# The way into the seven products: S blocks rounded ahead of the silu, rests in the order of use, one output half moved up

## The chip, the cores and the metric

The kernel runs on one core of one Trainium2 chip. The metric is the device time of the whole program in microseconds (us). Before the change three runs gave 2737.22, 2741.45 and 2741.87 us, median 2741.45 us.

## What is computed

Two blocks in sequence over 512 tokens of width 1024: a block with an HGRN/pool mixer and a forgetting-attention mixer, and a block with gated linear attention, retention and four SwiGLU feed-forward stages. The change lies in the feed-forward stages alone:

```
D_FF = 2816
def swiglu(x, w_in, w_out):
    gate, up = jnp.split(x @ w_in, 2, axis=-1)
    return (jax.nn.silu(gate) * up) @ w_out
# in second_block, twice for each of two layers:
h = layer_norm(DN_ALPHA * h + 0.5 * swiglu(h, ffn_w_in[i, j], ffn_w_out[i, j]), ...)
```

Everything is float32. The kernel makes a float32 product of three fast ones: each operand is rounded (its "hi"), the rest is the difference ("lo"), and hi\*hi + lo\*hi + hi\*lo are summed in PSUM.

## The kernel before

**Stages and rounds.** The four feed-forward stages are called ffn00, ffn01, ffn10 and ffn11. Each has ROUNDS = 11 rounds r; a round covers 256 hidden columns in two halves, s = 0 and 1, whose weights are the pieces a (s = 0) and b (s = 1). I write a2 for the piece a of round 2. The output weights of a round are its piece o; the products with them are issued one round later, so o1 is multiplied behind a2 and b2. Pieces are loaded by SyncE into a ring of SLOTS = 3 buffers (`sync_piece`, L300), a load waiting until the piece three places before has given its rests (`w_lo`).

**Two ways to multiply.** Rounds 0 and 1 are plain. From round SEVEN = 2 on, a half is seven block products after Strassen and Winograd (`tensor_seven`, L876) instead of eight: in the order of PRODUCTS (L835) A11, S2, S1, S3, A12, S4, A22, numbered x = 0 to 6. Each is 12 matmuls of 128 x 256. S1 to S4 are sums of weight blocks, made by GpSimd in `gpsimd_sums` (L985), four TENSOR_TENSORs at L991 to L996 that read and write SBUF. ScalarE rounds all four in one instruction (`scalar_unit_s`, L1021), VectorE makes the rests in two instructions of two blocks each (`vector_unit_s`, L1045) and then raises `w_s`. The sums of the next half may overwrite the one buffer `sums` only after that.

**Behind the products.** VectorE combines the products from PSUM: `vector_mid` step 0 gives f_u (L1065), step 1 gives f_e (L1068), step 2 gives f_g (L1071, L1072); product x = 4 waits for f_u, x = 5 for f_e, x = 6 for f_g. `vector_c11` (L1078) and `vector_c12` (L1084) finish two blocks, ScalarE takes their silu (`scalar_products`, L1115), and VectorE multiplies (`vector_products`, L1092 and twice L1097) and raises f_h. Then ScalarE rounds the hidden values (L542) and VectorE makes their rest (`vector_hidden_split`, L548), which sets oh_lo.

**Output products.** `tensor_out` (L436 to L438) makes eight tiles j of 6 matmuls of 128 x 512 in four PSUM banks. The first half of tiles 0 to 3 comes first, then their second half; tile 4 waits until VectorE has added tile 0 to the accumulator (`vector_outs_ffn`, L530 in round 1, L532 later, event acc), tile 5 waits for tile 1, and so on.

**What sets the order.** Every engine executes its instructions in the order written out by hand. For VectorE in the first seven-product round that is `vector_seventh` (L1216), for ScalarE the branch `r == SEVEN` in `scalar_ffn` (L1164). In this round (r = 2) the S blocks of a3 are rounded behind the silu of b2, and their rests are made behind the multiplications of b2; for b2 itself `tensor_seven` waits at x = 1 for `w_s`, that is for all four rests (L886). From round 3 on another loop takes over, which the change does not touch.

Of the kernel before, what the change touches and what calls it, by code (L numbers as in the profile page):

```python
# [7 lines left out]
F32 = mybir.dt.float32  # L8
# [6 lines left out]
MULT, ADD, SUB, MAX, MIN = ALU.mult, ALU.add, ALU.subtract, ALU.max, ALU.min  # L15

P = 128
T = 512
# [105 lines left out]
SEVEN = 2  # L124
# [113 lines left out]
def buffer(n):  # L238

    return n % SLOTS  # L240
# [103 lines left out]
def vector_piece_half(k, n, c):  # L344
    k.nc.vector.wait_ge(*k.at("w_hi", n))
    x = slice(c * D, (c + 1) * D)
    ins = k.nc.vector.tensor_tensor(k.lo(n)[:, x], k.w_raw[:, buffer(n), x], k.hi(n)[:, x].bitcast(F32), SUB)
    if c == 1:
        ins.then_inc(*k.up("w_lo", n))
# [479 lines left out]

H_BLOCK = {"B11": (0, 0), "B12": (0, 1), "B21": (1, 0), "B22": (1, 1)}  # L830
T_BLOCK = {"T2": 0, "T4": 1, "T3": 2}
S_BLOCK = {"S3": 0, "S1": 1, "S4": 2, "S2": 3}


PRODUCTS = (("A11", "B11", 0), ("S2", "T2", 1), ("S1", "T1", 2), ("S3", "T3", 3),  # L835
# [40 lines left out]
def tensor_seven(k, stage, r, s):  # L876

    pe, n, prior = k.nc.tensor, AT[stage, "ab"[s], r], before_seven(stage, r, s)
    pe.wait_ge(*k.at("w_lo", n))
    for x, (a, b, bank) in enumerate(PRODUCTS):  # L880
        if x < 4:
            event = ("f_p1", "f_c11", "f_c12", "f_c21")[x]
            pe.wait_ge(*(k.at(event, prior) if prior else k.at("f_h", (stage, r - 1, 1))))
        else:
            pe.wait_ge(*k.at(("f_u", "f_e", "f_g")[x - 4], (stage, r, s)))
        if x == 1 and r == SEVEN:  # L886
            pe.wait_ge(*k.at("w_s", n))
        if x == 1 and not prior:
            pe.wait_ge(*k.at("t_lo", (stage, "T3")))
        if x == 2 and not prior:  # L890
            pe.wait_ge(*k.at("t_lo", (stage, "T1")))
        (wh, wl), (xh, xl) = w_block(k, n, a), h_block(k, stage, b)
        for kk in range(4):
            w = slice(kk * P, (kk + 1) * P)
            ins = three(k, k.bank[bank][:, 0:256], wh[:, w], wl[:, w], xh[:, kk, :], xl[:, kk, :],
                        kk == 0, kk == 3)
        if x < 6:
            ins.then_inc(*k.up("f_p", (stage, r, s, x)))
    ins.then_inc(*k.up("used", n))
# [107 lines left out]
def scalar_unit_a22(k, n):  # L1007
    sc = k.nc.scalar
    sc.wait_ge(*k.at(f"loaded{buffer(n)}", n))
    sc.wait_ge(*k.at("used", BEFORE[n]))  # L1010
    sc.activation(wide_view(w_blocks(k, n, "A22", 1)[0]), raw_block(k, n, 1, 1), ACT.Copy
                  ).then_inc(*k.up("u_hi", (n, "A22")))


def scalar_unit_s(k, n):

    sc, (stage, what, r) = k.nc.scalar, PIECES[n]
    sc.wait_ge(*k.at("sums", n))
    if what == "a" and r > SEVEN:
        sc.wait_ge(*k.at("f_p", (stage, r - 1, 1, 1)))  # L1020
    sc.activation(w_blocks(k, n, "S", 4)[0], k.sums, ACT.Copy).then_inc(*k.up("u_hi", (n, "S")))  # L1021
# [12 lines left out]
def vector_unit_a22(k, n):  # L1034
    ve = k.nc.vector
    ve.wait_ge(*k.at("u_hi", (n, "A22")))
    hi, lo = (wide_view(x) for x in w_blocks(k, n, "A22", 1))
    ve.tensor_tensor(lo, raw_block(k, n, 1, 1), hi.bitcast(F32), SUB)


def vector_unit_s(k, n, half):
    ve, x = k.nc.vector, slice(half * 2 * T, (half + 1) * 2 * T)
    ve.wait_ge(*k.at("u_hi", (n, "S")))
    hi, lo = (w[:, x] for w in w_blocks(k, n, "S", 4))
    ins = ve.tensor_tensor(lo, k.sums[:, x], hi.bitcast(F32), SUB)  # L1045
    if half:
        ins.then_inc(*k.up("w_s", n))


def vector_unit_a1(k, n):  # L1050
# [24 lines left out]
def vector_c11(k, stage, r, s):  # L1075
    ve, key, p1 = k.nc.vector, (stage, r, s), k.f_h[:, s, HALF[0]]
    ve.wait_ge(*k.at("f_p", key + (4,)))
    ve.tensor_tensor(p1, p1, k.bank[1][:, 0:256], ADD).then_inc(*k.up("f_c11", key))  # L1078
# [30 lines left out]
def scalar_products(k, stage, r, s):  # L1109

    sc, key = k.nc.scalar, (stage, r, s)
    for t in range(2):
        sc.wait_ge(*k.at(("f_c11", "f_c12")[t], key))
        x = k.f_h[:, s, HALF[t]]
        sc.activation(x, x, ACT.Silu).then_inc(*k.up(("f_x1", "f_x2")[t], key))  # L1115
# [18 lines left out]
def scalar_ffn(k, stage):  # L1134
    sc, B = k.nc.scalar, FFN_NEXT[stage]
    sc.preload_act_table(ACT.Silu)
    scalar_piece(k, AT[stage, "a", 1])
    scalar_t(k, stage, "T2")
    scalar_hidden(k, stage, 0, 0)
    scalar_piece(k, AT[stage, "b", 1])  # L1140
    scalar_hidden_split(k, stage, 0, 0)
    scalar_t(k, stage, "T4")
    scalar_hidden(k, stage, 0, 1)
    scalar_hidden_split(k, stage, 0, 1)
    scalar_piece(k, AT[stage, "o", 0])
    scalar_t(k, stage, "T3")
    scalar_hidden(k, stage, 1, 0)
    n = AT[stage, "a", SEVEN]
    scalar_unit_a22(k, n)
    scalar_hidden_split(k, stage, 1, 0)  # L1150
    scalar_hidden(k, stage, 1, 1)
    scalar_unit_s(k, n)
    scalar_hidden_split(k, stage, 1, 1)
    scalar_unit_a1(k, n)
    scalar_t(k, stage, "T1")
    n = AT[stage, "b", SEVEN]
    scalar_unit_a22(k, n)
    for r in range(SEVEN, ROUNDS):
        last = r == ROUNDS - 1
        if r > SEVEN:  # L1160
            scalar_piece(k, AT[stage, "o", r - 1])
        scalar_first(k, stage, r, 0)
        scalar_unit_a1(k, AT[stage, "b", r])
        if r == SEVEN:  # L1164
            scalar_piece(k, AT[stage, "o", r - 1])
            scalar_unit_s(k, n)
            scalar_products(k, stage, r, 0)
            scalar_first(k, stage, r, 1)
            scalar_hidden_split(k, stage, r, 0)
            n = AT[stage, "a", r + 1]  # L1170
            scalar_unit_a22(k, n)
            scalar_products(k, stage, r, 1)
            scalar_unit_s(k, n)
            scalar_hidden_split(k, stage, r, 1)
            scalar_unit_a1(k, n)
            n = AT[stage, "b", r + 1]
            scalar_unit_a22(k, n)
            scalar_unit_s(k, n)
            continue
        scalar_products(k, stage, r, 0)  # L1180
        scalar_hidden_split(k, stage, r, 0)
        if not last:
            n = AT[stage, "a", r + 1]
            scalar_unit_a22(k, n)
            scalar_first(k, stage, r, 1)
            scalar_unit_s(k, n)
        else:
            scalar_first(k, stage, r, 1)
            scalar_piece(k, AT[stage, "o", r])
        scalar_products(k, stage, r, 1)  # L1190
        if last:
            sc.preload_act_table_set(EXP_LN)
        scalar_hidden_split(k, stage, r, 1)
        if not last:
            scalar_unit_a1(k, n)
            n = AT[stage, "b", r + 1]
            scalar_unit_a22(k, n)
            scalar_unit_s(k, n)
        elif B != "end":
            scalar_piece(k, HEAD[B][0])  # L1200
            scalar_piece(k, HEAD[B][1])
    scalar_exit(k, B)
# [9 lines left out]
def vector_hidden_split(k, stage, r, s):  # L1212
    vector_split(k, s, k.f_h[:, s, :], (stage, r, s), *ffn_oh(k, stage, r))


def vector_seventh(k, stage):  # L1216


    r = SEVEN
    n, n_o = AT[stage, "b", r], AT[stage, "o", r - 1]  # L1220
    vector_unit_a22(k, n)
    vector_mid(k, stage, r, 0, 0)
    vector_mid(k, stage, r, 0, 1)
    vector_unit_a1(k, n)
    vector_mid(k, stage, r, 0, 2)
    vector_piece_half(k, n_o, 0)
    vector_c11(k, stage, r, 0)
    vector_unit_s(k, n, 0)
    vector_c12(k, stage, r, 0)
    vector_unit_s(k, n, 1)  # L1230
    vector_products(k, stage, r, 0)
    k.nc.vector.wait_ge(*k.at("f_h", (stage, r, 0)))
    vector_mid(k, stage, r, 1, 0)
    vector_hidden_split(k, stage, r, 0)
    vector_mid(k, stage, r, 1, 1)
    vector_piece_half(k, n_o, 1)
    vector_mid(k, stage, r, 1, 2)
    n = AT[stage, "a", r + 1]
    vector_unit_a22(k, n)
    vector_c11(k, stage, r, 1)  # L1240
    vector_c12(k, stage, r, 1)
    vector_products(k, stage, r, 1)
    vector_unit_s(k, n, 0)
    vector_unit_s(k, n, 1)
    vector_hidden_split(k, stage, r, 1)
    vector_outs_ffn(k, stage, r - 1, range(2))
    vector_unit_a1(k, n)
    vector_outs_ffn(k, stage, r - 1, range(2, 4))
    n = AT[stage, "b", r + 1]
    vector_unit_a22(k, n)  # L1250
    vector_unit_s(k, n, 0)
    vector_outs_ffn(k, stage, r - 1, range(4, 6))
    vector_unit_s(k, n, 1)
    vector_outs_ffn(k, stage, r - 1, range(6, 8))
# [2315 lines left out]
```

## Time and profile before

| | us |
|---|---|
| median of three runs | 2741.45 |
| lowest, highest run | 2737.22, 2741.87 |
| span of the profiled execution | 2737.2 |
| TensorE matmul busy | 2660.2 (97%) |
| VectorE busy | 1940.6 (71%) |
| ScalarE busy | 1067.6 (39%) |
| GpSimd busy | 579.8 (21%) |
| mean granted TensorE clock | 0.994 |

The profiled execution is as long as the lowest of the three runs; nothing measurable lies around its span. Busy time of TensorE is the union of its matmuls, which overlap, so a pause shows best as the distance between the starts of two neighbours. In a timeline row the first number is the start in us from the start of the span, the second the duration, and a bracket at the end names idle time in front and what ended it. The engines are PE (TensorE), DVE (VectorE), ACT (ScalarE), POOL (GpSimd).

### The profile page before, as it was taken

The numbers are of one execution on the slowest core, as the hardware profiler recorded it, in microseconds if no ns is written. First come the engines' busy times: TensorE is split into PE (matmuls) and PEld (weight loads), VectorE is DVE, ScalarE is ACT, GpSimd is POOL, SyncE is SP. The second block draws the span as 40 slices with busy tenths as digits, with TensorE's granted clock in tenths as the row PEclk, the third lists the DMA queues.
The fourth block names the chain that finished last, engine by engine and source line by source line (L and its number), as shares of the span: only waits on it lengthen the run. The fifth ranks groups of instructions, "written<-read, shape, count | busy, mean of one in ns | idle before, by whom it ended". The sixth has DMA issues, their size and how long they took to land.

```text
span 2737.2 us, 38521 instructions
## 1 busy us (share of the span) xinstructions
PE 2660.2 (97%) x15927; PEld 2302.7 (84%) x15927; DVE 1940.6 (71%) x2634; ACT 1067.6 (39%) x1518; POOL 579.8 (21%) x370
## 2 busy tenths in 40 slices
PE   7999999999999999999999999999999999999998
PEld 5778877678899998888899988999978778788997
DVE  6888744556887875448888788888744644888887
ACT  4444455553443335343333334433322222344342
POOL 2111000011434300001444214433000000044430
PEclk9999999999999999999999999999999999999999
DMA  8444221212333332221433323332423213233331
GB/s 278 141 145 125 78 62 62 63 61 78 95 122 93 107 94 78 93 62 62 124 93 111 113 71 123 93 108 93 135 77 108 76 65 106 62 108 93 97 119 47
DMA packets 289856, 268.32 MB, mean 98 GB/s; under 512 B 10566, under 2 KB 256592, under 8 KB 288400
## 3 DMA queue, kind: packets, MB, share of 16 engines
q1 hardware_dynamic: 286448, 256.98, 30.1%
q0 software_dynamic: 2368, 6.64, 0.7%
q8 instruction: 126, 2.06, 0.3%
q10 hardware_dynamic: 864, 2.23, 0.3%
q14 instruction: 50, 0.41, 0.0%
HBM read 263.72 MB, written 2.10 MB: 97 GB/s over the span
## 4 chain that ended last, share of the span: by engine, by line
PE 74%; DVE 16%; ACT 4%; issue 3%; POOL 1%; DMA 0%; SPq 0%; DVEq 0%; ACTq 0%; POOLq 0%
PE psum L355 13%; PE psum L357 12%; PE psum L356 12%; PE psum L436 6%; PE psum L437 6%; PE psum L438 6%; PE psum L413 2%; PE psum L415 2%; PE psum L414 2%; DVE w_lo L340 2%; DVE acc L532 2%; DVE w_lo L1045 1%; PE psum L3266 1%; DVE stat L681 1%; PE psum L2810 1%
## 5 line engine op out<-in xcount | busy, mean ns | idle before, releaser
L355 PE MATMUL psum<-h_hi,w_hi 128*128 128x256 f32 (+1 forms) x2288 | 739.0, 323 | 19.2 <-DVE f_cffn L1065 6.5
L357 PE MATMUL psum<-h_hi,w_lo 128*128 128x256 f32 (+1 forms) x2288 | 720.6, 315 | 0.0
L356 PE MATMUL psum<-h_lo,w_hi 128*128 128x256 f32 (+1 forms) x2288 | 720.3, 315 | 0.0
L355 PEld LDWEIGHTS psum<-h_hi,w_hi 128*128 128x128 f32 x2288 | 438.5, 192 | 54.8 <-issue 13.8
L356 PEld LDWEIGHTS psum<-h_lo,w_hi 128*128 128x128 f32 x2288 | 438.7, 192 | 28.7 <-issue 5.1
L357 PEld LDWEIGHTS psum<-h_hi,w_lo 128*128 128x128 f32 x2288 | 438.3, 192 | 27.1
L991 POOL TENSOR_TENSOR val<-w_raw 128x512 f32<-128x512 f32 x72 | 100.6, 1398 | 1353.6 <-DMA w_raw<-in_ffn_w_in 948.5
L340 DVE TENSOR_TENSOR w_lo<-w_raw,w_hi 128x2048 fp32r<-128x2048 f32 x101 | 229.6, 2286 | 150.7 <-ACT w_hi L335 141.2
L532 DVE SCALAR_TENSOR_TENSOR acc<-psum,acc 128x512 f32<-128x512 f32 x416 | 270.0, 679 | 43.4 <-PE psum L438 43.4
L335 ACT ACTIVATE w_hi<-w_raw 128x2048 fp32r<-128x2048 f32 x104 | 197.1, 1910 | 140.1 <-PE psum L438 69.0
L355 PE MATMUL psum<-t_hiffn,w_hi 128*128 128x256 f32 x864 | 245.2, 284 | 3.4 <-DVE w_lo L1045 2.2
L356 PE MATMUL psum<-t_loffn,w_hi 128*128 128x256 f32 x864 | 244.5, 283 | 0.0
L357 PE MATMUL psum<-t_hiffn,w_lo 128*128 128x256 f32 x864 | 244.5, 283 | 0.0
L1045 DVE TENSOR_TENSOR w_lo<-val,w_hi 128x1024 fp32r<-128x1024 f32 x144 | 174.6, 1215 | 24.9 <-ACT w_hi L1021 24.1
L1115 ACT ACTIVATE consts<-consts 128x256 f32<-128x256 f32 x144 | 58.3, 418 | 318.6 <-DVE consts L1078 298.7
L355 PEld LDWEIGHTS psum<-t_hiffn,w_hi 128*128 128x128 f32 x864 | 165.8, 192 | 4.9 <-issue 2.9
L356 PEld LDWEIGHTS psum<-t_loffn,w_hi 128*128 128x128 f32 x864 | 165.8, 192 | 0.0
L357 PEld LDWEIGHTS psum<-t_hiffn,w_lo 128*128 128x128 f32 x864 | 165.8, 192 | 0.0
L994 POOL TENSOR_TENSOR val<-w_raw 128x512 f32<-128x512 f32 x72 | 161.4, 2242 | 0.0
L1021 ACT ACTIVATE w_hi<-val 128x2048 fp32r<-128x2048 f32 x72 | 137.9, 1915 | 38.8 <-POOL val L996 32.3
L335 ACT ACTIVATE w_hiffn<-w_raw 128x2048 fp32r<-128x2048 f32 x40 | 76.5, 1912 | 128.6 <-PE psum L438 128.6
L436 PE MATMUL psum<-w_hiffn,f_oh_hiffn 128*128 128x512 f32 x320 | 125.8, 393 | 0.0
(433 smaller groups left out, 5431.9 us busy)
## 6 DMA issues: line engine op xcount, KB each, us to landing
w_raw<-in_ffn_w_in SPq DMA_DIRECT2D x176, 512.0 KB, 5.0
w_raw<-in_ffn_w_out SPq DMA_DIRECT2D x88, 512.0 KB, 6.2
w_raw<-in_ret_w_in SPq DMA_DIRECT2D x48, 512.0 KB, 4.6
ada_raw<-in_ada_w SPq DMA_DIRECT2D x32, 512.0 KB, 4.5
w_raw<-in_odd_w_in SPq DMA_DIRECT2D x32, 512.0 KB, 5.0
w_raw<-in_even_w_in SPq DMA_DIRECT2D x24, 512.0 KB, 7.1
w_raw<-in_gla_w_in SPq DMA_DIRECT2D x24, 512.0 KB, 4.7
ada_first<-in_ada_w SPq DMA_DIRECT2D x8, 1024.0 KB, 9.6
```

Source lines behind the costliest of these rows:

```text
L335: k.nc.scalar.activation(k.hi(n), k.w_raw[:, buffer(n), :], ACT.Copy).then_inc(*k.up("w_hi", n))
L340: k.nc.vector.tensor_tensor(k.lo(n), k.w_raw[:, buffer(n), :], k.hi(n).bitcast(F32), SUB).then_inc(*k.up("w_lo", n))
L355: k.nc.tensor.matmul(out, ws, xs, start=first, stop=False)
L356: k.nc.tensor.matmul(out, ws, xl, start=False, stop=False)
L357: return k.nc.tensor.matmul(out, wl, xs, start=False, stop=last)
L436: k.nc.tensor.matmul(o, hi[:, c, x], k.hi(n)[:, w], start=first, stop=False)
L437: k.nc.tensor.matmul(o, lo[:, c, x], k.hi(n)[:, w], start=False, stop=False)
L438: return k.nc.tensor.matmul(o, hi[:, c, x], k.lo(n)[:, w], start=False, stop=last)
L532: ins = k.nc.vector.scalar_tensor_tensor(dst, b, 1.0, dst, MULT, ADD)
L994: po.tensor_tensor(sum_block(k, "S3"), a11, a21, ADD).then_inc(*k.pool.up())
L1021: sc.activation(w_blocks(k, n, "S", 4)[0], k.sums, ACT.Copy).then_inc(*k.up("u_hi", (n, "S")))
L1045: ins = ve.tensor_tensor(lo, k.sums[:, x], hi.bitcast(F32), SUB)
```

## The change

Four things, all of them in or in front of round 2 or 3 of each feed-forward stage.

1. The blocks S1 to S4 lie in the order S3, S4, S1, S2, and `vector_unit_s` makes the rests of S1 and S2 first (step 0), then those of S3 and S4 (step 1). Each step raises `w_s`. In round 2 TensorE waits at x = 1 for step 0 and at x = 3 for step 1.
2. ScalarE rounds the S blocks of a3 ahead of the silu of b2.
3. VectorE makes the rests of a3's S blocks ahead of c11 and c12 of b2, and no longer behind the multiplications.
4. The second half of o1's rests (`vector_piece_half`) comes ahead of step 1 of `vector_mid` for b2, in the place of the rest of the first hidden half, which moves behind c12.

```
-S_BLOCK = {"S3": 0, "S1": 1, "S4": 2, "S2": 3}
+S_BLOCK = {"S3": 0, "S4": 1, "S1": 2, "S2": 3}
...
-        if x == 1 and r == SEVEN:
-            pe.wait_ge(*k.at("w_s", n))
+        if r == SEVEN and x in (1, 3):
+            pe.wait_ge(*k.at("w_s", (n, "S1 S2") if x == 1 else n))
...
-def vector_unit_s(k, n, half):
-    ve, x = k.nc.vector, slice(half * 2 * T, (half + 1) * 2 * T)
+def vector_unit_s(k, n, step):
+
+    ve, x = k.nc.vector, slice((1 - step) * 2 * T, (2 - step) * 2 * T)
     ve.wait_ge(*k.at("u_hi", (n, "S")))
     hi, lo = (w[:, x] for w in w_blocks(k, n, "S", 4))
-    ins = ve.tensor_tensor(lo, k.sums[:, x], hi.bitcast(F32), SUB)
-    if half:
-        ins.then_inc(*k.up("w_s", n))
+    ve.tensor_tensor(lo, k.sums[:, x], hi.bitcast(F32), SUB).then_inc(*k.up("w_s", n if step else (n, "S1 S2")))
...
             n = AT[stage, "a", r + 1]
             scalar_unit_a22(k, n)
+            scalar_unit_s(k, n)
             scalar_products(k, stage, r, 1)
-            scalar_unit_s(k, n)
             scalar_hidden_split(k, stage, r, 1)
...
     vector_mid(k, stage, r, 1, 0)
-    vector_hidden_split(k, stage, r, 0)
+    vector_piece_half(k, n_o, 1)
     vector_mid(k, stage, r, 1, 1)
-    vector_piece_half(k, n_o, 1)
     vector_mid(k, stage, r, 1, 2)
     n = AT[stage, "a", r + 1]
     vector_unit_a22(k, n)
+    vector_unit_s(k, n, 0)
+    vector_unit_s(k, n, 1)
     vector_c11(k, stage, r, 1)
     vector_c12(k, stage, r, 1)
+    vector_hidden_split(k, stage, r, 0)
     vector_products(k, stage, r, 1)
-    vector_unit_s(k, n, 0)
-    vector_unit_s(k, n, 1)
     vector_hidden_split(k, stage, r, 1)
     vector_outs_ffn(k, stage, r - 1, range(2))
     vector_unit_a1(k, n)
```

## Rows read from the trace of the kernel before

**Rows 1.** The page's busy times: engine, us, share of the span, instructions.
```profile
PE 2660.2 (97%) x15927; PEld 2302.7 (84%) x15927; DVE 1940.6 (71%) x2634; ACT 1067.6 (39%) x1518; POOL 579.8 (21%) x370
```

**Rows 2.** Waits of PE: waiting line, releaser, us in total, times, longest.
```profile
PE psum L355 <- DVE f_cffn L1065: 6.5, 4, 1.6
```

**Rows 3.** Timeline of PE, stage ffn00, rounds 2 and 3.
```profile
715.20 0.28 PE L355 MATMUL psum<-h_hi,w_hi 128*128 128x256 f32 x1
...
717.34 0.35 PE L355 MATMUL psum<-t_hiffn,w_hi 128*128 128x256 f32 x1 [0.55 <-DVE w_lo L1045]
...
718.85 0.28 PE L355 MATMUL psum<-h_hi,w_hi 128*128 128x256 f32 x1
...
720.29 0.28 PE L355 MATMUL psum<-t_hiffn,w_hi 128*128 128x256 f32 x1
...
725.07 0.39 PE L355 MATMUL psum<-t_hiffn,w_hi 128*128 128x256 f32 x1 [0.30 <-DVE f_cffn L1072]
...
732.19 0.50 PE L436 MATMUL psum<-w_hiffn,f_oh_hiffn 128*128 128x512 f32 x1
...
737.77 0.28 PE L355 MATMUL psum<-h_hi,w_hi 128*128 128x256 f32 x1
...
745.32 0.38 PE L355 MATMUL psum<-h_hi,w_hi 128*128 128x256 f32 x1 [1.64 <-DVE f_cffn L1065]
...
747.86 0.38 PE L355 MATMUL psum<-h_hi,w_hi 128*128 128x256 f32 x1 [0.85 <-DVE consts L1068]
...
751.02 0.39 PE L355 MATMUL psum<-h_hi,w_hi 128*128 128x256 f32 x1
```

**Rows 4.** Timeline of DVE, the same stretch.
```profile
714.52 1.21 DVE L1045 TENSOR_TENSOR w_lo<-val,w_hi 128x1024 fp32r<-128x1024 f32 x1
...
717.56 2.83 DVE L1097 SCALAR_TENSOR_TENSOR consts<-consts,f_cffn 128x256 f32<-128x256 f32 x2
720.42 0.42 DVE L1065 TENSOR_TENSOR f_cffn<-consts,psum 128x256 f32<-128x256 f32 x1
721.09 1.03 DVE L548 TENSOR_TENSOR oh_lo<-consts,oh_hi 128x512 fp32r<-128x512 f32 x1 [0.24 <-ACT oh_hi L542]
...
722.37 1.98 DVE L347 TENSOR_TENSOR w_loffn<-w_raw,w_hiffn 128x1024 fp32r<-128x1024 f32 x1
...
728.58 2.36 DVE L1045 TENSOR_TENSOR w_lo<-val,w_hi 128x1024 fp32r<-128x1024 f32 x2 [0.56 <-ACT w_hi L1021]
...
731.46 0.68 DVE L532 SCALAR_TENSOR_TENSOR acc<-psum,acc 128x512 f32<-128x512 f32 x1
...
740.19 1.23 DVE L1045 TENSOR_TENSOR w_lo<-val,w_hi 128x1024 fp32r<-128x1024 f32 x1 [4.53 <-ACT w_hi L1021]
```

**Rows 5.** Timeline of ACT, the same stretch.
```profile
720.42 0.63 ACT L542 ACTIVATE oh_hi<-consts 128x512 fp32r<-128x512 f32 x1 [3.15 <-DVE consts L1097]
...
726.64 1.91 ACT L1021 ACTIVATE w_hi<-val 128x2048 fp32r<-128x2048 f32 x1
```

**Rows 6.** Timeline of POOL, the same stretch.
```profile
717.35 1.31 POOL L991 TENSOR_TENSOR val<-w_raw 128x512 f32<-128x512 f32 x1 [4.93 <-DVE w_lo L1045]
...
720.07 1.50 POOL L994 TENSOR_TENSOR val<-w_raw 128x512 f32<-128x512 f32 x1
721.64 1.63 POOL L996 TENSOR_TENSOR val<-val,w_raw 128x512 f32<-128x512 f32 x1
...
731.08 1.62 POOL L991 TENSOR_TENSOR val<-w_raw 128x512 f32<-128x512 f32 x1 [7.81 <-DVE w_lo L1045]
```

**Rows 7.** Timeline of PE between two stages: a long pause.
```profile
1239.81 0.36 PE L355 MATMUL psum<-h_hi,w_hi 128*128 128x256 f32 x1 [2.24 <-DVE h_lo L595]
```

**Rows 8.** Windows: us, busy of PE, PEld, DVE, ACT, POOL; granted clock, DMA share, GB/s.
```profile
740.00:750.00 10.00, 7.51 (x61) 7.11 (x60) 9.71 (x12) 3.17 (x4) 5.96 (x4) 1.00 0.01 2
1239.00:1247.00 8.00, 7.20 (x47) 7.23 (x48) 7.67 (x12) 0.52 (x3) 0.00 (x0) 0.79 0.01 3
88.00:100.00 12.00, 10.73 (x50) 8.94 (x50) 6.54 (x13) 3.07 (x5) 0.00 (x0) 0.72 0.99 302
```

## The prediction

> **What bounds the kernel now.** I read the busy times first: TensorE is busy for 97% of the span [rows 1], so only its pauses and what takes their place can move the end. The waits of PE come next. The one for f_u has 6.5 us in four times, the longest 1.6 [rows 2]: once in each of the four stages, and the longest is the mean, so the stages repeat. The timeline of PE in one stage then shows where: all pauses lie between the second half of round 2 (b2) and the second half of round 3 (b3) [rows 3]. Two starts without a pause, 718.85 and 720.29, give 1.44 us for a product of 12 matmuls; 717.34 to 718.85 is one with a restart (1.51), so a restart costs about 0.1. The 24 output matmuls from 732.19 to 737.77 take 5.58, restart included, 0.228 each. The pauses, restart included, from start to start:
> - 715.20 to 717.34 is 2.14 for one product: 0.70 lost (S rests of b2).
> - 717.34 to 725.07 is 7.73 for five products of 1.44: 0.53 lost (f_g of b2).
> - 725.07 to 737.77 is 12.70 for one product (1.44) and the 48 output matmuls, which run every 0.228 us (10.94): 0.32 lost, partly restarts, partly tile 4 of the output waiting for VectorE's addition, which ended at 732.14 [rows 4].
> - 737.77 to 745.32 is 7.55 for four products: 1.79 lost (f_u of a3). 745.32 to 747.86: 1.10 lost (f_e). 747.86 to 751.02: 0.28 lost, and 0.10 to restart behind it.
> The sum is 4.8 us a stage, 19.3 us in all. That is the most the change could bring. The 1.79 has a chain behind it: VectorE's rests of a3's S blocks (728.58) free GpSimd to make the sums of b3 (731.08), and VectorE sat idle for 4.53 us until these were rounded (740.19) [rows 4, 6]. The change pulls this chain forward.
>
> **How GpSimd and VectorE meet.** All that follows hangs on this. VectorE's first multiplication (717.56, two of them in 2.83 us) and GpSimd's sums (717.35) run together [rows 4, 6]. GpSimd's instruction at 720.07 ends at 721.57, and VectorE's rest, begun at 721.09, ends at 722.12, 0.55 behind it. GpSimd's next begins at 721.64 and ends at 723.27, 1.15 behind that, and the half of o1's rests (722.37) ends at 724.35, 1.08 behind that. An instruction of the one waits until that of the other has ended, then takes its own time: about 1.16 for a GpSimd sum, 1.08 for 1024 columns on VectorE, 0.55 for 512, 0.29 for 256 (2.83 for two multiplications is two sums and twice 0.29 in turn). VectorE instructions that read PSUM keep their time beside GpSimd: f_u took 0.42 at 720.42.
> The Trainium skill says the same (SBUF: State Buffer, section "SBUF: two separate sides"): the pair of ports is an exclusive lock for the whole instruction and not a split of bandwidth, for VectorE instructions with two SBUF inputs. If they split it and each ran at half its rate, the chain below would end 1.35 us earlier in each stage and the sum would be 5.4 us less.
>
> **Part by part, in stage ffn00, on the clock of the kernel before.**
> (1) S rests in the order of use. The first half of b2's rests ends at 715.73 (714.52 + 1.21 [rows 4]), product x = 1 can start at 716.64: the 0.70 goes. The second half is needed at x = 3, 719.52, and ended in front of 717.35. Raising `w_s` twice adds no wait: nothing.
> (2) The output half. VectorE has f_u at 720.84 as before, and x = 4 wants it at 720.96. Then comes the half of o1's rests: GpSimd's third sum holds until about 721.55, so it ends at 722.63. f_e follows at 722.96, while TensorE wants x = 5 at 722.40: a new pause of 0.61 and 0.10 for the restart. The 0.53 at x = 6 goes, since f_g comes at 723.62 and is wanted at 724.5. Output tiles start at 726.0, not 726.6. GpSimd's fourth sum is pushed behind the same half and ends at 723.80, not 723.27. o1's rests are ready 1.7 us earlier, and SyncE starts the load of o2 that much earlier; its reader comes after round 2.
> (3) ScalarE's rounding of a3's sums begins at 723.84 in place of 726.64 [rows 5] and takes 1.91: 725.78. The silu queues behind it, but c11, which it waits for, is queued behind the S rests on VectorE anyway: nothing.
> (4) VectorE: S rests of a3 725.78 to 728.14 (2.36 [rows 4]), 2.8 us earlier than before. From there GpSimd starts the sums of b3, at 728.28 and not 731.08 [rows 6], and this is what collides. c11 and c12 read PSUM and end at 728.80. The moved rest of the first hidden half waits for the first sum (729.57) and ends at 730.12. c21 (PSUM) to 730.46. Multiplication one waits for the second sum (730.12 + 1.16 = 731.28) and ends at 731.57; multiplication two for the third (732.73), ends at 733.02. ScalarE rounds, 0.63 [rows 5], to 733.69. The rest of the second half waits for the fourth sum (733.02 + 1.16 = 734.18) and ends at 734.74. The first output tile is added from 734.66 for 0.68 [rows 4] to 735.34. In the kernel before, the same addition began at 731.46: GpSimd was idle from 723.27 to 731.08 (7.81 [rows 6]), so that the multiplications of b2 ran alone. Without the sums beside them this stretch would be about 3 us shorter.
> (5) Who waits for that: TensorE at tile 4. It would have wanted it at 732.1 before (725.07 + 1.44 + 0.1 + 24 x 0.228) and got it at 732.19; now it wants it at 731.47 and gets it at 735.39. New pause: 3.92, and 0.11 for the restart.
> (6) What goes in exchange. a3 starts at 735.39 + 5.58 (737.77 less 732.19) = 740.97. The sums of b3 are ready at 734.2, their rounding ends about 737.0, the rests are made at about 740.0 and 742.4 between the output additions, f_u at 744.5 against a want of 746.73, f_e at the latest at 747.7 against 748.17. So 1.79, 1.10, 0.28 and the last 0.10 all go. SyncE's load of a4 waits for a3's A1 rests, which come 3.2 us later (737.1); GpSimd reads a4 only after b3's rests at 742.4. If that cover failed, sums would be late that no product needs before round 4.
> Sum for a stage: new pauses 0.71 + 4.03 = 4.74 against 4.82. Gain about 0.1, 0.4 us in all four. Pulling the chain forward is paid back by its collision.
>
> **The clock.** A pause of 3.9 us is longer than any in the middle of the kernel. Around 1239.81 PE had paused for 2.24 us behind another 1.2 us pause and a few transposes [rows 7], and the granted clock of 1239 to 1247 was 0.79 [rows 8]: 0.21 x 8 us is 3.4 us at the lower level (1.2 for 2.4 GHz), which costs half of it, 1.7 us. The pauses of 1.64 and 0.85 us in the stage left it alone (1.00 in 740 to 750). Bounds for a stage: 0 and 1.7; nearer to the upper end, since 3.9 is above the pause that brought it down; some of the slow stretch may fall into the pause itself. I take 1.4, 5.6 us in four stages.
> The Trainium skill has a rule against this change here (TensorE: Matmul & The Clock Gate, section "What's actually happening"): the low clock is the default and activity releases it. By the rule each of the four pauses brings the clock down; without the rule the sum is 5.6 us less. The row agrees for the pause it shows.
>
> **The time.** On the profiled execution: 2737.2 - 0.4 + 5.6 = 2742.4 us. That execution is the lowest of the three; the median lies 4.2 above. Part of such a spread may be falls of the clock at the pauses that go away, so I carry over half: 2744.5 us, 0.1% above the median of before.
>
> **The rivals.**
> - Slower: the clock falls in full, and longer. In 88 to 100 the granted clock was 0.72 [rows 8], 0.28 x 12 / 0.5 = 6.7 us at the lower level, a price of 3.4. With 1.7 to 3.4 a stage the sum is 2737.2 - 0.4 + 6.8 to 13.6 = 2743.6 to 2750.4, and with the median's 4.2, 2747.8 to 2754.6. It decides from about 1.4 a stage when the whole 4.2 carries over. For it: each pause is nearly twice the one of 1239.81. Against: that one was followed by 3.4 us only.
> - The clock stays up: 2736.8 on the profiled execution, up to 2741.0 with the 4.2. For it: 1.64 did not bring it down. Against: 2.24 did.
> - No collision: GpSimd's sums of b3 start later (the data of b3 are late) or give way. The pause at tile 4 is then about 1.0 and a stage loses 0.71 + 1.05 = 1.76: 3.1 gained, 12.4 in all, 2724.8, or 2729.0 on the median's basis. Against: b3's buffer is free from 717.35 on, and GpSimd started at once behind the same signal before [rows 6]. If they share evenly, it is 5.4 less than the forecast, with a shorter pause and less clock: about 2735.
> - The change doesn't do what it says: the earlier rounding waits for something else and the order of before comes back. Then 2741, no change.
>
> **How the numbers follow.** Forecast 0.42, slower rival 0.25, clock stays up 0.15, no or mild collision 0.13, no effect 0.05. A measurement of this kernel can tell about 0.2% (5.5 us) from no change, so the bounds are 2736.0 and 2746.9. Faster: the collision rival and a little of the steady clock, 0.18. Slower: the slower rival and a part of the forecast, 0.30. Same: 0.52. The range is 2731 to 2752: it leaves out the full gain and the longest low clock.
>
> **What would show it.** In the changed kernel's waits of PE: f_u and w_lo L1045 gone, f_e (L1068) four times 0.6 in b2, and L436 <- DVE acc L532 with four times about 3.7. The two multiplications (L1097) behind b2's c21 take 2.5 us, as the two at 717.56 do. POOL L991 of b3 starts behind the S rests of a3 by 0.14. The mean granted clock falls by 0.002 to 0.005. It is wrong if tile 4 waits under 2 us, if GpSimd and VectorE alternate otherwise than shown, or if f_u of a3 still has a pause.

## The result

The changed kernel has a median of 2745.88 us over 11 runs (2739.37 to 2749.43), the kernel before on the same chips 2739.14 us (11 runs). The ratio is 1.0024, 95% interval 1.0016 to 1.0032: slower by 0.24%, 6.7 us between the medians. The span of the profiled execution is 2746.4 us, 9.2 us longer than that of before. It belongs to the run of 2747.87 us, the second longest of the eleven.

The page of the changed kernel has the same shares as [rows 1]; TensorE is busy 6.7 us longer:

```profile
PE 2666.9 (97%) x15927; PEld 2310.3 (84%) x15927; DVE 1947.4 (71%) x2634; ACT 1068.5 (39%) x1518; POOL 568.8 (21%) x370
```

Its waits of PE, beside [rows 2] (waiting line, releaser, us in total, times, longest). The waits for f_u are gone. The wait for an output addition, which stood elsewhere with 3.3 us in four times, now has 18.0 in eight; the four new ones are 3.7 each:

```profile
PE psum L436 <- DVE acc L532: 18.0, 8, 3.7
...
PE psum L355 <- DVE consts L1067: 1.7, 4, 0.4
```

The timeline of PE in stage ffn00, beside [rows 3]. This execution runs 1.58 us later at this place, so subtract 1.58 to come to the clock of before. f_e is waited for at 724.60, output tile 4 at 736.87; two lines further the distance from start to start goes from 0.227 to 0.43 us:

```profile
724.60 0.39 PE L355 MATMUL psum<-h_hi,w_hi 128*128 128x256 f32 x1 [0.44 <-DVE consts L1067]
...
732.58 0.39 PE L437 MATMUL psum<-w_hiffn,f_oh_loffn 128*128 128x512 f32 x1
732.81 0.39 PE L438 MATMUL psum<-w_loffn,f_oh_hiffn 128*128 128x512 f32 x1
736.87 0.50 PE L436 MATMUL psum<-w_hiffn,f_oh_hiffn 128*128 128x512 f32 x1 [3.67 <-DVE acc L532]
737.21 0.40 PE L437 MATMUL psum<-w_hiffn,f_oh_loffn 128*128 128x512 f32 x1
737.45 0.52 PE L438 MATMUL psum<-w_loffn,f_oh_hiffn 128*128 128x512 f32 x1
737.76 0.63 PE L436 MATMUL psum<-w_hiffn,f_oh_hiffn 128*128 128x512 f32 x1
738.19 0.63 PE L437 MATMUL psum<-w_hiffn,f_oh_loffn 128*128 128x512 f32 x1
```

The timeline of DVE behind it, beside [rows 4]. The half of o1's rests takes 1.89, the rests of a3's S blocks begin at 727.33, and then three instructions in a row are stretched: the moved rest of the first hidden half (1.43), the two multiplications (2.48) and the rest of the second half (0.98). The addition comes at 736.14:

```profile
722.33 1.89 DVE L347 TENSOR_TENSOR w_loffn<-w_raw,w_hiffn 128x1024 fp32r<-128x1024 f32 x1
...
727.33 2.36 DVE L1046 TENSOR_TENSOR w_lo<-val,w_hi 128x1024 fp32r<-128x1024 f32 x2 [1.33 <-ACT w_hi L1021]
729.61 0.41 DVE L1077 TENSOR_TENSOR consts<-consts,psum 128x256 f32<-128x256 f32 x1
729.94 0.41 DVE L1083 TENSOR_TENSOR consts<-consts,psum 128x256 f32<-128x256 f32 x1
730.27 1.43 DVE L548 TENSOR_TENSOR oh_lo<-consts,oh_hi 128x512 fp32r<-128x512 f32 x1
731.63 0.41 DVE L1091 TENSOR_TENSOR f_cffn<-f_cffn,psum 128x256 f32<-128x256 f32 x1
732.07 2.48 DVE L1096 SCALAR_TENSOR_TENSOR consts<-consts,f_cffn 128x256 f32<-128x256 f32 x2
735.24 0.98 DVE L548 TENSOR_TENSOR oh_lo<-consts,oh_hi 128x512 fp32r<-128x512 f32 x1 [0.70 <-ACT oh_hi L542]
736.14 1.27 DVE L532 SCALAR_TENSOR_TENSOR acc<-psum,acc 128x512 f32<-128x512 f32 x2
```

ScalarE's rounding of a3's S blocks (beside [rows 5]) and GpSimd's four sums of b3 (beside [rows 6]). Each stretched instruction of VectorE ends just behind one of GpSimd's: 731.70 behind 731.16, 734.55 behind 734.26, 736.22 behind 735.67:

```profile
725.38 1.91 ACT L1021 ACTIVATE w_hi<-val 128x2048 fp32r<-128x2048 f32 x1 [2.24 <-POOL val L996]
```

```profile
729.84 1.32 POOL L991 TENSOR_TENSOR val<-w_raw 128x512 f32<-128x512 f32 x1 [4.48 <-DVE w_lo L1046]
731.23 1.62 POOL L993 TENSOR_TENSOR val<-val,w_raw 128x512 f32<-128x512 f32 x1
732.81 1.45 POOL L994 TENSOR_TENSOR val<-w_raw 128x512 f32<-128x512 f32 x1
734.34 1.33 POOL L996 TENSOR_TENSOR val<-val,w_raw 128x512 f32<-128x512 f32 x1
```

The windows around the pause in each of the four stages, beside the 1.00 of 740 to 750 in [rows 8] (us; busy of PE, PEld, DVE, ACT, POOL; granted clock, DMA share, GB/s):

```profile
730.00:742.00 12.00, 8.33 (x30) 6.37 (x29) 11.27 (x15) 4.65 (x6) 5.51 (x4) 0.86 0.18 52
1325.00:1340.00 15.00, 11.32 (x38) 8.77 (x37) 13.95 (x19) 4.65 (x6) 5.86 (x5) 0.77 0.26 70
1683.00:1698.00 15.00, 11.34 (x39) 8.78 (x38) 13.95 (x18) 4.65 (x6) 5.68 (x4) 0.77 0.25 70
2459.00:2474.00 15.00, 11.31 (x39) 8.80 (x39) 14.02 (x19) 4.65 (x6) 5.94 (x5) 0.77 0.25 70
```

0.14 x 12 / 0.5 is 3.4 us at the lower level (1.2 for 2.4 GHz) in the first stage, 0.23 x 15 / 0.5 is 6.9 in each of the other three; part of it lies in the pause. So the pauses of a stage are about as long as before (the old ones gone, a new one of 3.8 to 3.9 and one of 0.7 in their place), and the clock comes on top. From b2 to the end of b3, start to start of the matmuls, a stage takes 46.0 us before (45.7 in ffn10), and 47.4 (ffn00), 48.6 (ffn01, ffn10) and 48.3 (ffn11) now. That is 9.2 us more in all, the whole difference of the two spans. In ffn00, with the output products at full clock, it would be 45.8.

### The profile page after: what moved, and what is told of

The parts are those of the page before. It is cut to its first block, busy times and chain, and to the rows that moved or that the text cites. A ratio compares the mean times of both kernels' runs of the same rounds, so it can differ in the third digit from the quotient of the medians.

```text
span 2746.4 us, 38529 instructions
## 1 busy us (share of the span) xinstructions
PE 2666.9 (97%) x15927; PEld 2310.3 (84%) x15927; DVE 1947.4 (71%) x2634; ACT 1068.5 (39%) x1518; POOL 568.8 (21%) x370
## 4 chain that ended last, share of the span: by engine, by line
PE 76%; DVE 16%; ACT 4%; issue 2%; POOL 1%; DMA 1%; SPq 0%; DVEq 0%; POOLq 0%; ACTq 0%
PE psum L355 13%; PE psum L357 13%; PE psum L356 13%; PE psum L436 7%; PE psum L437 6%; PE psum L438 6%; PE psum L413 2%; PE psum L415 2%; PE psum L414 2%; DVE w_lo L340 2%; DVE acc L532 1%; PE psum L3265 1%; DVE stat L681 1%; PE psum L2809 1%; DVE acc L691 1%
## 5 line engine op out<-in xcount | busy, mean ns | idle before, releaser
L991 POOL TENSOR_TENSOR val<-w_raw 128x512 f32<-128x512 f32 x72 | 99.0, 1375 | 1373.6 <-DMA w_raw<-in_ffn_w_in 970.7
L532 DVE SCALAR_TENSOR_TENSOR acc<-psum,acc 128x512 f32<-128x512 f32 x416 | 270.8, 680 | 45.7 <-PE psum L438 45.7
L994 POOL TENSOR_TENSOR val<-w_raw 128x512 f32<-128x512 f32 x72 | 156.0, 2167 | 0.0
L436 PE MATMUL psum<-w_hiffn,f_oh_hiffn 128*128 128x512 f32 x320 | 130.0, 406 | 14.7 <-DVE acc L532 14.7
```

Of the source, the lines that this page charges most:

```text
L436: k.nc.tensor.matmul(o, hi[:, c, x], k.hi(n)[:, w], start=first, stop=False)
L532: ins = k.nc.vector.scalar_tensor_tensor(dst, b, 1.0, dst, MULT, ADD)
L994: po.tensor_tensor(sum_block(k, "S3"), a11, a21, ADD).then_inc(*k.pool.up())
```

## The experiments

The theory on test has two parts. (a) Pulling the sums of b3 forward makes them collide with VectorE's multiplications, and that, not the order as such, holds back the first output addition. (b) The long pause at one place brings the granted clock down where about the same length in several pieces did not. Each kernel ran beside the kernel before on the same chip; the first four share one chip, with a median before of 2738.63 us (33 runs), the last four another, with 2738.3 us (15 runs). A ratio is always to the kernel before on that chip.

### One part alone: S rests in the order of use

```
 (kernel before)
+S_BLOCK = {"S3": 0, "S4": 1, "S1": 2, "S2": 3}
...
+        if r == SEVEN and x in (1, 3):
+            pe.wait_ge(*k.at("w_s", (n, "S1 S2") if x == 1 else n))
... (vector_unit_s is that of the changed kernel)
```

> The kernel before with the first part of the change alone: S1 and S2 first, and the waits of TensorE split over x = 1 and x = 3. Theory: the 0.70 us in front of x = 1 of b2 goes, but f_g of b2 comes from VectorE's queue at 725.0 whatever TensorE does, so the pause in front of x = 6 grows from 0.5 to about 1.2 and nothing is gained: 2739.1 us, ratio 1.000. Rival: the pauses of a stage are independent and add up; then 4 x 0.70 = 2.8 us are gained, 2736.3, ratio 0.999, and the pause in front of x = 6 stays at 0.5.

2738.8 us (11 runs), ratio 1.0002 (0.9993 to 1.0011). The wait for the S rests is gone from the waits of PE, and the one for f_g has 3.5 us in four times. Its timeline shows the pause at x = 6 of b2 at 0.89, where [rows 3] has 0.30:

```profile
726.68 0.39 PE L355 MATMUL psum<-t_hiffn,w_hi 128*128 128x256 f32 x1 [0.89 <-DVE f_cffn L1071]
```

VectorE sets the end of this pause at a time that does not hang on TensorE, so the pause took up what was saved ahead of it. The theory held: this part alone gains nothing. The rival's 0.9990 lies just outside the interval, and its pause of 0.5 is not what the row shows.

### One part alone: ScalarE rounds ahead of the silu

```
 (kernel before)
             scalar_unit_a22(k, n)
+            scalar_unit_s(k, n)
             scalar_products(k, stage, r, 1)
-            scalar_unit_s(k, n)
```

> The kernel before with ScalarE's new order alone (S blocks of a3 rounded ahead of the silu of b2), VectorE's order as it was. Theory: VectorE no longer sits idle for 0.56 us before a3's rests, w_s and all that hangs on it come about 0.6 us earlier, the multiplications still run with GpSimd idle; the pause at f_u of a3 shrinks by 0.6 and the 0.1 at output tile 4 goes: 0.7 a stage, 2736.3 us, ratio 0.999, clock unchanged. Rival: the silu pays for it, c21 and the multiplications of b2 come later and eat the 0.6: ratio 1.000 or above.

2736.28 us, ratio 0.9993 (0.9984 to 1.0001). The waits for f_u fell from 6.5 to 5.0 us in all:

```profile
PE psum L355 <- DVE f_cffn L1065: 5.0, 4, 1.2
```

The size is that of the theory (2.4 us between the medians, 2.8 expected), but the interval touches 1: the time alone doesn't settle it. The trace does: the four stages take 45.4, 45.1, 45.4 and 45.3 us in place of 46.0, 46.0, 45.7 and 46.0, 2.6 less in all. The silu did not pay. This execution runs 2.09 us later at this place (f_u of b2 at 722.51, in [rows 4] at 720.42). The silu begins at 728.07, as soon as c11 has come; in the kernel before it began at 725.98, just 2.09 earlier:

```profile
728.07 0.75 ACT L1115 ACTIVATE consts<-consts 128x256 f32<-128x256 f32 x2 [0.76 <-DVE consts L1078]
```

Of the two parts that were tried alone, this one shortens the stage: it uses the slack of ScalarE and leaves VectorE's order as it was.

### The collision taken away

```
 (changed kernel, gpsimd_ffn)
+            if (r, s) == (SEVEN + 1, 1):
+                k.nc.gpsimd.wait_ge(*k.at("oh_lo", (stage, SEVEN, 1)))
             gpsimd_sums(k, stage, r, s)
```

> The changed kernel, but GpSimd starts the sums of b3 only when the rest of b2's hidden half (oh_lo) is made, so that nothing collides with VectorE between a3's S rests and the first output addition. Collision theory: each of the two multiplications takes 0.4 us again, tile 4 waits about 0.9 us in place of 3.8, the granted clock stays up, and the pauses at f_u and f_e of a3 (1.8 and 1.1) come back since the sums of b3 are as late as before the change: 4.9 us of pauses a stage, 2739.6 us, ratio to before 1.000. Rival, the order alone: what delays tile 4 is that the S rests stand ahead of the additions in VectorE's queue; then tile 4 still waits over 3 us, the clock falls, and with f_u back the time is 2750 or more.

2743.22 us, ratio 1.0013 (1.0004 to 1.0022). The decisive lines are those of VectorE and PE in ffn00. With GpSimd idle, the rest of the first hidden half takes 0.68, the two multiplications 0.76, and tile 4 waits 0.93 us, not 3.67:

```profile
729.67 0.68 DVE L548 TENSOR_TENSOR oh_lo<-consts,oh_hi 128x512 fp32r<-128x512 f32 x1
730.27 0.41 DVE L1091 TENSOR_TENSOR f_cffn<-f_cffn,psum 128x256 f32<-128x256 f32 x1
730.72 0.76 DVE L1096 SCALAR_TENSOR_TENSOR consts<-consts,f_cffn 128x256 f32<-128x256 f32 x2
```

```profile
733.52 0.50 PE L436 MATMUL psum<-w_hiffn,f_oh_hiffn 128*128 128x512 f32 x1 [0.93 <-DVE acc L532]
...
746.80 0.44 PE L355 MATMUL psum<-h_hi,w_hi 128*128 128x256 f32 x1 [1.79 <-DVE f_cffn L1064]
747.03 0.42 PE L356 MATMUL psum<-h_lo,w_hi 128*128 128x256 f32 x1
```

The order is that of the changed kernel, so the order alone is not what delays tile 4; part (a) stands. The pause at f_u is back at 1.79, as expected. The forecast of 2739.6 was 3.6 us too low, and the windows show why: the granted clock in the stretches of a3 and b3 was 0.83 in ffn00, 1.00 in ffn01, 0.66 in ffn10 and 0.83 in ffn11. It fell in three of four stages, which the expectation had excluded: in ffn00 in the pause at f_u (the two matmuls above start 0.23 apart, 0.12 at full clock), in ffn11 just behind it, in ffn10 only at the pause at f_e. A stage takes 46.5 us in ffn01, and 46.7, 48.8 and 46.8 in the other three: 2.9 us for the clock in all.

```profile
743.00:753.00 10.00, 8.21 (x55) 7.96 (x55) 8.88 (x14) 2.44 (x5) 7.48 (x4) 0.83 0.04 10
1340.00:1350.00 10.00, 7.74 (x60) 7.33 (x61) 9.16 (x14) 1.88 (x5) 8.05 (x4) 1.00 0.16 46
1698.00:1708.00 10.00, 9.16 (x55) 8.95 (x55) 7.39 (x11) 1.68 (x4) 6.46 (x3) 0.66 0.35 98
2472.00:2482.00 10.00, 8.38 (x55) 8.09 (x56) 9.14 (x15) 1.58 (x4) 8.09 (x4) 0.83 0.16 45
```

This speaks against the simple form of part (b). The pauses of this kernel are split up again (0.7, 1.1, 1.95 and, where the clock had not fallen yet, 1.1 us lost), much as in the kernel before, and the clock fell all the same. Splitting a pause is no guard by itself.

### The first two additions ahead of the multiplications

```
 (changed kernel, vector_seventh)
     vector_hidden_split(k, stage, r, 0)
+    vector_outs_ffn(k, stage, r - 1, range(2))
     vector_products(k, stage, r, 1)
     vector_hidden_split(k, stage, r, 1)
-    vector_outs_ffn(k, stage, r - 1, range(2))
     vector_unit_a1(k, n)
```

> The changed kernel with the additions of output tiles 0 and 1 ahead of c21 and the multiplications of b2 on VectorE. Theory: tile 0 is added by 730.8, TensorE wants it at 731.5, so the pause at tile 4 (3.8) and the fall of the clock both go, and the pauses at f_u and f_e of a3 stay away; what is left is the 0.7 at f_e of b2. 4.1 us less than before in a stage, 16.4 in all: 2722.7 us, ratio 0.994. The multiplications still take 2.5 us beside the sums, which then costs nothing. Rival: the later hidden half of b2 (rests at about 735.5, a3's A1 rests at 736.7) takes the place of the pause, in front of a3 (wanted at 736.9) or at f_u: then a new pause of 1 us or more stands there and the gain is under 12 us.

2742.85 us, ratio 1.0013 (1.0005 to 1.0022): a miss by 20 us, and neither theory nor rival had it. The pause is nearly as long as in the changed kernel (3.6 us lost in place of 3.8), but two tiles later:

```profile
736.31 0.80 PE L436 MATMUL psum<-w_hiffn,f_oh_hiffn 128*128 128x512 f32 x1 [3.44 <-DVE acc L532]
```

The multiplications and the second hidden half still stand ahead of the additions of tiles 2 and 3, which tiles 6 and 7 wait for, and this execution's VectorE timeline has them at 735.57, against 728.56 for the first two. I had followed the releaser of tile 4 and not that of tile 6. The mechanism of the theory was right (the delayed addition sets the pause), its address was wrong.

The clock adds something on part (b). With the same 3.6 us lost in each stage it fell in three of the four and not in ffn11, where the output products with their pause took 14.7 us, against 17.1, 16.2 and 15.8:

```profile
735.00:747.00 12.00, 10.69 (x55) 9.53 (x56) 9.24 (x12) 4.96 (x4) 5.55 (x4) 0.72 0.32 89
1331.00:1343.00 12.00, 10.31 (x62) 9.43 (x63) 10.31 (x12) 5.35 (x5) 5.16 (x4) 0.86 0.32 87
1688.00:1700.00 12.00, 10.31 (x62) 9.47 (x63) 10.31 (x12) 5.34 (x5) 5.07 (x4) 0.86 0.32 89
2462.00:2474.00 12.00, 9.85 (x71) 9.32 (x72) 11.48 (x17) 5.80 (x6) 4.76 (x3) 1.00 0.32 88
```

### The first two additions between the multiplications and the hidden rest

```
 (changed kernel, vector_seventh)
     vector_products(k, stage, r, 1)
+    vector_outs_ffn(k, stage, r - 1, range(2))
     vector_hidden_split(k, stage, r, 1)
-    vector_outs_ffn(k, stage, r - 1, range(2))
     vector_unit_a1(k, n)
```

> The changed kernel with the additions of output tiles 0 and 1 between the multiplications of b2 and the rest of its hidden half. This sets the pause at tile 4 to a middle length: tile 0 is added about 1.7 us earlier, so tile 4 waits 2.2 us and not 3.8, tile 6 at most 0.1. Pauses of a stage 3.1 us against 4.8 before: 7 us gained with the clock up, 2731.7. On the clock: if a pause lowers it by its length alone, 2.2 us is as long as the one that brought it down between two stages, and it falls in some of the four stages, mean granted clock 0.991 to 0.993, 2735 us, ratio 0.999. Rival: the clock falls with the pause of any length over 2 in all four stages as in the changed kernel; then 2740 or more.

2733.67 us, ratio 0.9985 (0.9976 to 0.9993), against 1.0024 for the changed kernel: about 11 us less for moving two additions past one instruction. Tile 4 waits 2.0 us (2.1 to 2.2 lost), and the granted clock of the four windows around it was 1.00, 0.83, 1.00 and 1.00:

```profile
735.00:745.00 10.00, 8.02 (x42) 6.34 (x41) 10.00 (x14) 5.46 (x5) 2.77 (x3) 1.00 0.38 105
1328.00:1338.00 10.00, 8.23 (x33) 6.84 (x34) 10.00 (x14) 4.70 (x5) 2.41 (x3) 0.83 0.38 105
1680.00:1692.00 12.00, 10.03 (x47) 7.84 (x47) 11.97 (x17) 5.27 (x7) 5.67 (x4) 1.00 0.27 77
2455.00:2468.00 13.00, 11.01 (x68) 9.52 (x67) 12.88 (x17) 7.16 (x7) 5.32 (x4) 1.00 0.31 81
```

The traces tell pause and clock apart. The output products take 13.4 us in the three stages with the clock up and 14.8 in ffn01, so the clock costs 1.4 us in place of 9.7. The four stages are 14.0 us shorter than in the changed kernel's profiled execution: 8.3 for the clock, the rest for the pauses. The spans differ by 11.3, so 2.7 of it is lost again outside these stages. Of part (b) this stands: the longer pause at this place brings the clock down more often, one of four stages at 2.1 us lost, four of four at 3.8. These are four stages of one execution each, and length is not all, as the two experiments ahead of this one show.

### The output half put one place back

```
 (changed kernel, vector_seventh)
-    vector_piece_half(k, n_o, 1)
     vector_mid(k, stage, r, 1, 1)
+    vector_piece_half(k, n_o, 1)
```

> The changed kernel with its moved output half put one place back, behind f_e of b2. The 0.6 us pause in front of x = 5 of b2 goes. Theory: tile 4 is released by VectorE at a time that does not hang on TensorE, so that pause grows by the same 0.6 and nothing is gained: ratio to before 1.002 as in the changed kernel, tile 4 waits about 4.3 us. Rival: pauses add up, 2.4 to 2.8 us are gained, 2743, ratio 1.001.

2746.85 us (5 runs), ratio 1.0035 (1.0022 to 1.0047), no better than the changed kernel, whose interval it overlaps. The wait for f_e is gone, and tile 4 waits 4.38 us in place of 3.67:

```profile
737.21 0.50 PE L436 MATMUL psum<-w_hiffn,f_oh_hiffn 128*128 128x512 f32 x1 [4.38 <-DVE acc L532]
```

The 0.7 moved and did not go, as in the first experiment; the clock fell in all four stages again (0.86 in 12 us, and 0.77 in 15 us of each of the other three). The rival's ratio of 1.001 lies below the interval.

### Four additions ahead, and then the rests of o2 late

```
 (kernel of the last experiment, vector_seventh; r = 2)
+    vector_outs_ffn(k, stage, r - 1, range(4))
     vector_hidden_split(k, stage, r, 0)
     vector_products(k, stage, r, 1)
+    vector_unit_a1(k, n)
     vector_hidden_split(k, stage, r, 1)
-    vector_outs_ffn(k, stage, r - 1, range(2))
-    vector_unit_a1(k, n)
-    vector_outs_ffn(k, stage, r - 1, range(2, 4))
     n = AT[stage, "b", r + 1]
     vector_unit_a22(k, n)
+    vector_outs_ffn(k, stage, r - 1, range(4, 6))
     vector_unit_s(k, n, 0)
-    vector_outs_ffn(k, stage, r - 1, range(4, 6))
     vector_unit_s(k, n, 1)
 (scalar_ffn: scalar_unit_a1(k, n) ahead of scalar_hidden_split(k, stage, r, 1))
```

> The same, and VectorE now adds output tiles 0 to 3 straight behind c12 of b2, ahead of everything that GpSimd's sums of b3 can hold up; a3's A1 rests ahead of the second hidden half; tiles 4 and 5 ahead of b3's S rests. The run before showed that with only tiles 0 and 1 ahead, tile 6 waits 3.6 us for the addition of tile 2. Theory: no pause at the output tiles and none in b2, no fall of the clock there; f_u of a3 comes just in time, but VectorE has a backlog: the rests of o2 (2.3 to 3.4 us) stand between f_u and f_e, so f_e leaves 1 to 2 us. 3 us a stage gained: 2727 us, ratio 0.996. Rival: the backlog moves the whole pause to f_u and f_e, ratio 0.999 or above.

2727.3 us (5 runs), ratio 0.9962 (0.9948 to 0.9975), as expected to 0.3 us. No pause is left in b2 and at the output tiles; f_e of a3 waits 1.62 us in ffn00 (0.83 in ffn10) behind the rests of o2:

```profile
741.76 3.06 DVE L340 TENSOR_TENSOR w_loffn<-w_raw,w_hiffn 128x2048 fp32r<-128x2048 f32 x1
744.74 0.41 DVE L1067 TENSOR_TENSOR consts<-f_cffn,psum 128x256 f32<-128x256 f32 x1
```

The second kernel puts that line behind c11 of a3:

```
 (vector_ffn, round 3 only)
         vector_mid(k, stage, r, 0, 0)
-        vector_piece(k, AT[stage, "o", r - 1])
         vector_mid(k, stage, r, 0, 1)
         vector_mid(k, stage, r, 0, 2)
         vector_unit_a1(k, AT[stage, "b", r])
         vector_c11(k, stage, r, 0)
+        vector_piece(k, AT[stage, "o", r - 1])
         vector_c12(k, stage, r, 0)
```

> The same as the one with four additions, and in round 3 the rests of o2 stand behind f_g and c11 and not between f_u and f_e. Theory: with the backlog's last long instruction out of the way f_e is in time too, pauses of a stage under 0.7 us in all, no fall of the clock in the stages: 16 to 17 us gained, 2722 us, ratio 0.994. Rival: what was 0.3 in front of b3 (its A1 rests) or c12 of a3 becomes the pause, and the gain is no larger than without this edit.

2724.0 us (5 runs), ratio 0.9947 (0.9935 to 0.9960): 14 us below the kernel before and, by the ratios, 21 below the changed one; 2722 was expected. A stage from b2 to the end of b3 takes 42.0 us (42.7 in ffn10), against 43.5 (42.4) in the kernel without this edit. The times of these two kernels have intervals that overlap, so only the traces separate them. One pause is left, at f_u of b3, 0.4 to 0.5 us in three stages and 1.17 in ffn10, where the forecast of under 0.7 did not hold:

```profile
754.61 0.39 PE L355 MATMUL psum<-h_hi,w_hi 128*128 128x256 f32 x1 [0.44 <-DVE f_cffn L1064]
```

So pulling the S blocks forward does pay, once the additions no longer stand behind the collision: three quarters of the 19.3 us that the prediction gave as the most.

## Why the prediction was right

**The bound and the pauses.** The largest possible gain was put at 4.8 us a stage, 19.3 in all. The last kernel took 4.0 of it in ffn00 (46.0 to 42.0) and 15.1 in the four stages. The pauses of the changed kernel, without the clock, came to 0.5 us less than before in all; 0.4 was forecast.

**(1) Order of use.** "The 0.70 goes": it went, but the first experiment shows that alone it is worth nothing.

**(2) The output half.** The new pause at f_e was put at 0.61 and a restart of 0.10. The row has 0.44 idle, 0.60 lost from start to start, and the restart behind it.

**(3), (4) Pull and collision.** On the clock of before, ScalarE's rounding was to begin at 723.84 and began at 723.80. The S rests were to begin at 725.78, and did at 725.75; the sums of b3 at 728.28, and did at 728.26; the first addition was to be at 734.66 and was at 734.56. The lock, read from a few pairs of rows, carried the whole chain with an error of 0.1 us. The experiment without the collision gives its price: 3.67 less 0.93 is 2.7 us of idle at tile 4; the prediction said about 3.

**(5) Tile 4.** Forecast 3.92 lost and 0.11 for the restart, measured 3.84 (3.82 to 3.85 over the four stages) and a restart of 0.11.

**(6) In exchange.** f_u, f_e and the A1 rests no longer stop TensorE in round 3: right.

**The clock.** This is the term that was too small. 1.4 us a stage were taken out of bounds of 0 and 1.7. The output products took 16.5 us in ffn00, 17.7 in ffn01, 17.6 in ffn10 and 17.3 in ffn11; at full clock they take 10.9 and the pause 3.9 to 4.0, so the clock cost 1.6, 2.8, 2.8 and 2.5 us, 9.7 in all. The upper bound of the forecast was wrong: it came from a pause of 2.24 us, and behind a longer one the clock was down for 6.9 us in three of four stages. The slower rival had just this (1.7 to 3.4 a stage) and deserved more than its 0.25. With the measured prices the sum on the profiled execution is 2737.2 - 0.5 + 9.7, or 2746.4, the measured span. This execution is one of the longer ones, though: its mean granted clock is 0.989, that of the other ten 0.990 to 0.993, and the shortest run, 2739.37 us, has 0.993. From the 6.7 us between the medians, an estimate of the usual price is 7.2 us in all, 1.8 a stage.

**The base.** I took the span of the profiled execution for its whole time. The executions profiled later show about 1.4 us around it, so that this one took about 2738.6 us (an estimate), close to the 2739.14 of eleven runs; the median of three lay 2.3 us above the median of eleven. Carrying over half of the 4.2 us put the base at 2739.3, right to 0.2 us. That the half came out is luck: it was a choice, and its reason, falls of the clock at the pauses that go away, is not shown. On this base 5.2 us more were forecast and 6.7 measured; the 1.5 that are missing are the clock's, and 2744.5 came out 1.4 below the measured median. The +0.1% was reckoned from the median of three; measured were 0.24%, just over the bound of 0.2%, on the side that had a chance of 0.30.

## What to carry to other kernels

Before a step is pulled forward, look at what it releases: here it started GpSimd's sums 2.8 us earlier, into the stretch in which VectorE's multiplications had run without them. Follow every consumer that stands behind the moved work in the queue, down to the last tile, and not only the first one that waits. A pause that ends at a time set by another engine can't be shortened from its front. And a long pause can cost more than itself, since the granted clock may fall with it; shorter ones escaped this in some kernels here and not in others, so a gain should be read with the clock of every stage beside it.

## What the runs showed of the hardware

The granted clock depended on how the pauses lay, more finely than I had expected. By the time lost from start to start, in the four stages of one execution each:

| kernel | pauses of a stage in order, us lost | stages in which the clock fell |
|---|---|---|
| before | 0.7, 0.5, 0.3, 1.8, 1.1 | 0 of 4 |
| four additions ahead | 1.0 to 1.9 | 0 of 4 |
| sums held | 0.7, 1.1, 1.95, 1.1 | 3 of 4 |
| additions between | 0.7, 2.1 | 1 of 4 |
| additions first | 0.7, 3.6 | 3 of 4 |
| changed | 0.7, 3.8 | 4 of 4 |
| half back | 4.5 | 4 of 4 |

In the changed kernel the same pause was followed by 3.4 us at the lower level in one stage and by 6.9 in the others, part of it inside the pause. Why 1.8 and 1.9 left the clock alone where 1.95 did not, and what sets the stages of one kernel apart, these runs don't show.

VectorE and GpSimd took turns, one instruction each, where both had work that needed the lock. The two multiplications (732.07, 2.48 us, 2.47 to 2.48 in all four stages) stand next to each other in VectorE's queue. They began before GpSimd's second sum had ended (732.85) and ended 0.29 us behind its third (734.26), which leaves room for one multiplication behind it: the third sum had its turn between the two. The Trainium skill (SBUF — State Buffer, section "SBUF: two separate sides") states the lock: whichever starts first has the shared ports for its whole instruction, and the other waits. The rows agree: VectorE's three stretched instructions end 0.54, 0.29 and 0.55 us behind GpSimd's.
